# All weight remainders in one GpSimd loop, and the 31-tap convolution with 13 taps on TensorE and its diagonals made on ScalarE

## The reference, cut to what matters

```python
def conformer_conv(x, pw1_w, pw1_b, dw_w, dw_b, ln_g, ln_b, pw2_w, pw2_b):
    h = x @ pw1_w + pw1_b
    a, g = jnp.split(h, 2, axis=-1)
    h = a * jax.nn.sigmoid(g)
    h = causal_dwconv(h, dw_w, dw_b)      # depthwise, 31 taps
    h = layer_norm(h, ln_g, ln_b)
    h = jax.nn.silu(h)
    return h @ pw2_w + pw2_b

def conv_gated_ffn(x, w_up, w_gate, conv_w, conv_b, w_down):
    u = x @ w_up
    g = causal_dwconv(x @ w_gate, conv_w, conv_b)   # depthwise, 3 taps
    return (jax.nn.silu(g) * u) @ w_down
```

## Time and profile before

| what | value |
| --- | --- |
| median of 3 executions | 2216.51 us (2215.62 to 2216.83) |
| the profiled execution | 2214.47 us |
| its span, first to last instruction | 2212.7 us |
| TensorE matmul busy | 2047.4 us, 93% |
| VectorE busy | 1145.1 us, 52% |
| ScalarE busy | 716.4 us, 32% |
| GpSimd busy | 146.0 us, 7% |
| mean granted TensorE clock | 0.964 |

### The profile page before, as it was taken

One profiled execution on the slowest core, in us unless ns is written; L12 is line 12 of the kernel. 1 busy time (PEld: TensorE's weight loads), 2 busy tenths in 40 slices (PEclk: granted clock), 3 DMA queues, 4 the chain that ended last, 5 costly groups with the idle time before them and its releaser, 6 DMA issues.

```text
span 2212.7 us, 22972 instructions
## 1 busy us (share of the span) xinstructions
PE 2047.4 (93%) x8878; PEld 1604.9 (73%) x8878; DVE 1145.1 (52%) x1315; ACT 716.4 (32%) x793; POOL 146.0 (7%) x200
## 2 busy tenths in 40 slices
PE   2998999999999699679999999989999999999996
PEld 0874678877788477456888888758777778888884
DVE  6674333225533799765455553354366545555433
ACT  2423233235422311145222231154365342222222
POOL 0000000000000388500000000000000000000000
PEclk8898999999999899889999999989999999999998
DMA  7211122221122011111222223212200222222221
GB/s 312 77 58 38 56 77 96 95 95 39 41 100 107 19 57 57 48 57 56 77 96 96 103 104 108 101 51 102 76 1 18 88 76 85 103 97 95 102 107 38
DMA packets 24831, 177.55 MB, mean 80 GB/s; under 512 B 2752, under 2 KB 2880, under 8 KB 4288
## 3 DMA queue, kind: packets, MB, share of 16 engines
q1 hardware_dynamic: 23040, 160.95, 20.4%
q10 hardware_dynamic: 1728, 15.73, 1.7%
HBM read 174.57 MB, written 2.10 MB: 80 GB/s over the span
## 4 chain that ended last, share of the span: by engine, by line
PE 81%; DVE 8%; issue 4%; ACT 4%; POOL 2%; DMA 1%; DVEq 0%; ACTq 0%; SPq 0%; POOLq 0%
PE PS L423 22%; PE PS L424 21%; PE PS L425 21%; PE PS L498 3%; PE PS L778 2%; POOL DG L390 2%; PE PS L788 2%; PE PS L489 1%; PE PS L488 1%; PE PS L487 1%; DVE WL L1157 1%; PE PS L606 1%; DVE ADAS L1225 1%; DVE TT L1180 1%; DMA SWR<-w_small 1%
## 5 line engine op out<-in xcount | busy, mean ns | idle before, releaser
L423 PE MATMUL PS<-H,WH 128*128 128x512 f32 x1552 | 614.2, 396 | 24.8 <-DVE L L1185 14.0
L424 PE MATMUL PS<-L,WH 128*128 128x512 f32 x1552 | 608.4, 392 | 0.0
L425 PE MATMUL PS<-H,WL 128*128 128x512 f32 x1552 | 608.0, 392 | 0.0
L1157 DVE TENSOR_TENSOR WL<-RAW,WH 128x2048 fp32r<-128x2048 f32 x149 | 341.3, 2290 | 325.7 <-ACT WH L817 325.2
L817 ACT ACTIVATE WH<-RAW 128x2048 fp32r<-128x2048 f32 x149 | 284.5, 1909 | 282.6 <-PE PS L425 238.0
L423 PEld LDWEIGHTS PS<-H,WH 128*128 128x128 f32 x1552 | 294.2, 190 | 94.0 <-issue 25.3
L425 PEld LDWEIGHTS PS<-H,WL 128*128 128x128 f32 x1552 | 293.9, 189 | 62.4
L424 PEld LDWEIGHTS PS<-L,WH 128*128 128x128 f32 x1552 | 294.1, 190 | 60.0 <-issue 0.2
L390 POOL TENSOR_SCALAR DG<-IDENT,DWC 128x128 fp32r<-128x128 f32 x176 | 142.6, 829 | 773.2 <-DVE DWC L1517 773.2
L423 PE MATMUL PS<-FH,WH 128*128 128x512 f32 x352 | 136.9, 389 | 0.0
L424 PE MATMUL PS<-FL,WH 128*128 128x512 f32 x352 | 136.9, 389 | 0.0
(11 more groups left out here) (284 smaller groups left out, 2622.6 us busy)
## 6 DMA issues: line engine op xcount, KB each, us to landing
RAW<-w SPq DMA_DIRECT2D x149, 1024.0 KB, 4.8
ADA<-w_ada ACTq DMA_DIRECT2D x8, 1536.0 KB, 23.8
X<-x_t SPq DMA_DIRECT2D x1, 2048.0 KB, 15.1
PWR<-w_ple ACTq DMA_DIRECT2D x2, 1024.0 KB, 4.8
out<-X SPq DMA_DIRECT2D x8, 256.0 KB, 2.2
PR<-p_t ACTq DMA_DIRECT2D x2, 512.0 KB, 5.9
PAR<-par SPq DMA_DIRECT2D x1, 334.0 KB, 7.0
SWR<-w_small SPq DMA_DIRECT2D x1, 160.0 KB, 18.8
```

Source lines behind the costliest of these rows:

```text
L423: nc.tensor.matmul(ps, wh, xh, start=start, stop=False)
L424: nc.tensor.matmul(ps, wh, xl, start=False, stop=False)
L425: return nc.tensor.matmul(ps, wl, xh, start=False, stop=stop)
L1157: v.tensor_tensor(WL[:, p], RAW[:, p], WH[:, p].bitcast(F32), ALU.subtract).then_inc(w_lo, 1)
```

## The change

The remainders of all 149 slots move from VectorE to GpSimd, in one loop that waits for the high part and subtracts. Nothing else runs on GpSimd behind its constants. The diagonals move from GpSimd to ScalarE, as activations with the weight column as scale, ahead of the slot's sigmoid; they are 26 a group now, as TensorE takes 13 taps and VectorE 18. The copy `DWC` is gone, and `CVB` and `DW` lie elsewhere.

```diff
-PE_TAPS = 11
+PE_TAPS = 13
...
-            def diagonals(s):
-                p = s.odd()
-
-                pool.wait_ge(dwc_ready, s.val(1, 1))
-                for part in range(2):
-                    for k in range(PE_TAPS):
-                        ins = nc.gpsimd.tensor_scalar(DG[:, p, part, k, :], IDENT[:], DWC[:, p, part, k:k + 1], None,
-                                                      ALU.mult)
-                ins.then_inc(dg_ready, 1)
-            for m in range(KC):
-                diagonals(Step(m))
+            def split_lo(g, p):
+                pool.wait_ge(w_hi, g + 1)
+                nc.gpsimd.tensor_tensor(WL[:, p], RAW[:, p], WH[:, p].bitcast(F32), ALU.subtract).then_inc(w_lo, 1)
+
+            with pool.Fori(0, NSLOTS // 2) as t:
+                for i in range(2):
+                    split_lo(2 * t + i, i)
+            for g in range(NSLOTS // 2 * 2, NSLOTS):
+                split_lo(g, g % 2)
...
+            def diagonals(s):
+                p = s.odd()
+                if not (isinstance(s.val(), int) and s.val() < 2):
+                    act.wait_ge(cp_ps, s.val(1, -1))
+                for part in range(2):
+                    for k in range(PE_TAPS):
+                        m = s.val(1, k * KC)
+                        w_ = DW[:, part, m:m + 1] if isinstance(m, int) else DW[:, part, bass.ds(m, 1)]
+                        ins = a(DG[:, p, part, k, :], IDENT[:], ACT.Identity, scale=w_.bitcast(F32))
+                ins.then_inc(dg_ready, 1)
+
             def pw1(s, p):
+                if isinstance(s.val(), int) and s.val() == 0:
+                    act.wait_ge(dw_lo, 1)
+                diagonals(s)
                 gates("pw1", KC, "pw1_b")(s, p)
...
-            slots("pw1", pw1)
+            slots("pw1", pw1, head=2)
...
             def slots(stage, body, per=0, tail=0, head=0):
-                g0 = SLOT0[stage]
-
-                def one(s):
-                    split_lo(s, 1, g0 + 1)
-                    body(s, s.odd(1, GROUP0[stage]))
-                steps(dve, own, COUNT[stage], per, one, tail=tail, head=head)
+                steps(dve, own, COUNT[stage], per, lambda s: body(s, s.odd(1, GROUP0[stage])), tail=tail, head=head)
...
-                v.tensor_copy(DWC[:, q].unsqueeze(3), dw[:, :, :, m:m + 1] if isinstance(m, int) else
-                              dw[:, :, :, bass.ds(m, 1)]).then_inc(dwc_ready, 1)
```

More of the change, by code:

```diff
@@ L218, in build @@
         DG = at("DG", A + 36, [P, 2, 2, PE_TAPS, P], F32R)
-        CVB = at("CVB", A + 60, [P, 1, T])
-        DW = at("DW", A + 62, [P, 2, PE_TAPS * KC], F32R)
-        DWC = at("DWC", A + 66, [P, 2, 2, PE_TAPS])
+        CVB = at("CVB", A + 62, [P, 1, T])
+        DW = at("DW", A + 64, [P, 2, PE_TAPS * KC], F32R)
         HCH = at("HCH", A + 68, [P, 2, PAD + T], F32R)
@@ L314, in build @@
         mg_ready, mg_hi, mg_lo = sem("mg_ready"), sem("mg_hi"), sem("mg_lo")
-        hc_hi, hc_lo, dw_hi, dwc_ready, dg_ready, cp_ps = (sem(s) for s in (
-            "hc_hi", "hc_lo", "dw_hi", "dwc_ready", "dg_ready", "cp_ps"))
+        hc_hi, hc_lo, dw_hi, dw_lo, dg_ready, cp_ps = (sem(s) for s in (
+            "hc_hi", "hc_lo", "dw_hi", "dw_lo", "dg_ready", "cp_ps"))
         sele_ready = sem("sele_ready")
@@ L1150, in _ @@
             acc, tmp = TT[:, 2, :], TT[:, 3, :]
[L1152 to L1157, removed]
-            def slots(stage, body, per=0, tail=0, head=0):
-                g0 = SLOT0[stage]
-                def one(s):
-                    split_lo(s, 1, g0 + 1)
-                    body(s, s.odd(1, GROUP0[stage]))
-                steps(dve, own, COUNT[stage], per, one, tail=tail, head=head)
+            def slots(stage, body, per=0, tail=0, head=0):
+                steps(dve, own, COUNT[stage], per, lambda s: body(s, s.odd(1, GROUP0[stage])), tail=tail, head=head)
             def evacuated(s, stage, mul=1, more=0):
@@ L1230, in _ @@
                         own.did(ins)
-            split_lo(Step(0), 1, 0)
             def modulation(part):
@@ L1287, in _ @@
             v.scalar_tensor_tensor(E, U, -1.0, U, ALU.mult, ALU.min).then_inc(dt_u, 1)
-            split_lo(Step(0), 1, SLOT0["q"] + 1)
             dve.wait_ge(dt_e, 1)
@@ L1373, in _ @@
             dve.wait_ge(cb_ready, 2)
-            split_lo(Step(1), 1, SLOT0["q"] + 1)
             seg(0)
             for h in range(SSM_HEADS):
-                if h % KC == 1:
-                    split_lo(Step(2 + h // KC), 1, SLOT0["q"] + 1)
                 if h + 1 < SSM_HEADS:
@@ L1392, in _ @@
             dve.wait_ge(y_used, KC)
-            slots("z", lambda s, p: None)
             for j in range(COUNT["k"]):
-                split_lo(Step(j), 1, SLOT0["k"] + 1)
                 if j == 0:
@@ L1409, in _ @@
             slots("ssm_out", ssm_out)
-            slots("v", lambda s, p: None)
             n = NT * FOX_HEADS
@@ L1428, in _ @@
             for i in range(n + 1):
-                if i % KC == 2:
-                    split_lo(Step(i // KC), 1, SLOT0["za"] + 1)
                 if i < n:
@@ L1491, in _ @@
             dve.wait_ge(dw_hi, 1)
-            own.did(v.tensor_tensor(DW[:, 1, :], col("dw_w", 0, PE_TAPS * KC), DW[:, 0, :].bitcast(F32), ALU.subtract))
-            own.settle()
+            v.tensor_tensor(DW[:, 1, :], col("dw_w", 0, PE_TAPS * KC), DW[:, 0, :].bitcast(F32),
+                            ALU.subtract).then_inc(dw_lo, 1)
             own.did(v.memset(acc, 0.0))
@@ L1513, in pw1 @@
                 cv, hc = rows(CV, s.val(), 1), rows(HC, s.val(), 1)
-                q, m = s.odd(), s.val()
-                dw = DW[:].bitcast(F32).rearrange("p a (k m) -> p a k m", m=KC)
-                v.tensor_copy(DWC[:, q].unsqueeze(3), dw[:, :, :, m:m + 1] if isinstance(m, int) else
-                              dw[:, :, :, bass.ds(m, 1)]).then_inc(dwc_ready, 1)
+                q = s.odd()
                 dsts = (cv, CVB[:])
@@ L1639, in down_one @@
                 def down_one(s):
-                    for part in range(DOWN_S):
-                        split_lo(s, DOWN_S, SLOT0[down] + part + 1)
                     added(down, DOWN_S, DOWN_S - 1)(s, s.odd(1, GROUP0[down]))
@@ L1672, in _ @@
             slots("k1", k1_lo, head=COUNT["k1"])
-            slots("v1", lambda s, p: None)
             for i in range(SB_HEADS + 2):
```

## The result

The changed kernel takes 2245.68 us (median of 4 runs, 2241.38 to 2246.04), the kernel before 2216.07 (4 runs on the same chip, 2215.51 to 2216.83). The ratio is 1.0129, 95% interval 1.0111 to 1.0146: slower, by 29.6 us where 11.8 were forecast. The profiled execution has a span of 2244.3 us against 2212.7, at a granted clock of 0.959 of full speed against 0.964.

A forecast was written before the change was run, and what follows sets the result against it. TensorE, with a matmul in flight for 93% of the span, was taken as the bound, `pw1` as paced by VectorE. Terms of 15.4 + 3.8 + 4.4 + 4.6 + 2.3 - 18.7 = +11.8 us gave 2228 us, range 2204 to 2256.

The forecast's parts named there:

- Step 6: All other stages, including attention and state-space heads: no change; if the cover fails, 1 to 3 us at some five places.
- Term 1: `up0` and `up1`: remainder ready 0.7 us after the need, once in two slots, over 44 slots: +15.4 us.
- Terms 2 and 4: Later remainders delay TensorE: `xbc` +3.8 us; second slots of `gate0` and `gate1` +4.6 together, of `q1` +2.3.
- Term 3: The start: GpSimd's subtraction takes its turn amid VectorE's modulation sums, which wait: +4.4 us.
- Term 5: `pw1`: VectorE's group falls from 21.1 to 19.8 us and the wait for GpSimd's diagonals goes: -18.7 us.
- -32: `pw1`: the change in us at which TensorE bounds the stage, if GpSimd's turn is shorter or does not hold VectorE.
- Rival 1: GpSimd's subtraction takes under 4.1 us, so the `up` stages cost nothing at 3.8: 2203 us, chance 0.2.
- Rival 2: The subtraction takes 4.5 us but does not hold VectorE throughout; TensorE bounds `pw1`: 2214 us, chance 0.13.
- Rival 3: GpSimd needs 5.3 us or more, or ScalarE's diagonals over 0.6 us each: 2256 us and up, chance 0.14.
- the forecast's 2217 to 2246: Whole kernel, for a GpSimd subtraction of 4.2 to 5 us: 2217 to 2246 us, chance 0.5.
- 35 us for each us: Whole kernel: each us of GpSimd's subtraction time moves the sum by 35 us, as long as it is above 3.8.

The follow-up runs named there:

- e3: e1 with only the remainders of two slots in the state-space heads (q3 and z0) moved to GpSimd: 2198.03 us, ratio 0.9922.
- e10: e3 with GpSimd subtracting only 8 of 16 tiles in those two slots, the other halves keeping old values: 2190.8 us, ratio 0.9885.
- e2: e1 with the remainders of the 44 slots made in `up0` and `up1` moved to GpSimd: 2214.78 us, ratio 0.9995.
- e7: e2 with GpSimd subtracting only 8 of a slot's 16 tiles, the others keeping old values: 2192.48 us, ratio 0.989.
- e11: e1 with 11 taps on TensorE instead of 13, all remainders on VectorE: 2193.62 us, ratio 0.9895.
- e5: The changed kernel with GpSimd's loop begun only after VectorE's modulation sums: 2239.31 us, ratio 1.0095.
- e1: The changed kernel's convolution half alone: 13 taps on TensorE, diagonals on ScalarE, all 149 remainders on VectorE: 2189.94 us, ratio 0.9881.
- e4: e1 with only the eight remainders made in `pw1` moved to GpSimd: 2200.64 us, ratio 0.9931.
- e6: e1 with only the remainders made in `gate0` and `gate1` moved to GpSimd: 2196.9 us, ratio 0.9907.

## Why the prediction was wrong

The direction, the hold and the place of most of the loss were right; the size was not. By its own steps:

- **Step 6, "All else at nothing", failed.** It let the state-space part's held operations "stand in front of a TensorE that has queued matmuls". The queue is shorter than the hold: in the changed kernel and in e3 TensorE waits 2.8 us for the held product and then loses 2.9 at the low clock, so that one hold costs 5.7 us (the changed kernel's stretch is 6.6 longer). The bound was named, 1 to 3 us at each of some five places, and taken as zero. e10 shows that it is the length of the turn: at 2.39 us all but 0.6 is gone.
- **Term 1, `up0` and `up1`, was mis-sized**: +15.4 forecast, +22.7 measured; e2 alone has +22.5. The mechanism stood: a delay per pair of slots, and only above the room (e7). But it is 1.07 us instead of 0.7. The subtraction is 4.60 us and not 4.5, and the two hand-overs take 0.08 and 0.13 instead of 0.1 together, so the product comes 0.9 after the need; and after a wait the second matmul comes 0.33 after the first instead of 0.23, in both slots. A few tenths of a microsecond, 22 times.
- **Terms 2 and 4 had the wait and not what follows it.** `xbc` +5.6 instead of +3.8, of which the low clock gives 1.7; the gates +6.2 instead of +4.6. Both waits grew by 2.3, as forecast; behind them the low clock took 2.8 more than before in `gate0` and 1.1 less in `gate1`. As e10 and e11 have the same 2.8 in `gate0` without the longer wait, this part can't be put down to the change. `q1` came out at +2.3 exactly. `xbc` was not tried alone, so its part rests on the trace.
- **Term 3, the start**: +4.7 against +4.4, and e5 takes it away, 4.7 us by the stage.
- **Term 5, `pw1`**: -20.0 against -18.7. The pace of 19.7 against 19.8 and the diagonals' 0.297 against 0.30 hold. The pace is in part luck: the parts that the text takes off 21.1 us sum to 5.5 and leave 15.6, not 15.3. The runs have 15.3 (17.5 in e1 less the 2.2 of the remainder), since without GpSimd's diagonals the taps come every 0.66 us instead of 0.78, more than the 0.09 a tap that was taken off. The two halves of the term are now separate: -26.2 for the convolution (e1), +6.2 for the turn of 4.6 us (e4). With no turn, e1 is at TensorE's 20.0 a group in its second half, so the "-32" of the text looks too much; its own case, with VectorE free of the remainders too, was not run.
- **Rival 1, a GpSimd under 4.1 us**, falls by every row of the subtraction. **Rival 2, no hold**, falls by the start, by `pw1` and by e3. **Rival 3** asked for 5.3 us or more: beside VectorE's taps it is 5.0 to 5.1 in the changed kernel (up to 5.5 in the gates, 7.0 once in `pw2`), 4.71 in the mean, and no stage was bound by ScalarE.
- **That 2245.7 lies inside the forecast's 2217 to 2246 is luck.** The upper end stood for a subtraction of 5 us. By the prediction's own rule, 35 us for each us, the measured 4.60 to 4.71 would give 2232 to 2235.

Between the profiled executions the sum was short by 19.8 us (31.6 less 11.8): 7.3 are term 1, 6.6 the heads of step 6, 3.4 terms 2 and 4, and 2.5 what is left of all other stretches. By the medians it was short by 17.8. The -3.0 of the attention and the +3.1 from `q1` to `wo` were not explained; they nearly cancel. Of the second, 1.3 lie in the third and fourth slots of `q1`, in `k1` and in the first slots of `v1`, and come back in e5 alone, the other kernel with all remainders on GpSimd. The rest lies in the attention behind them, which takes 129.0 to 133.1 us from kernel to kernel without such remainders.

## What to carry to other kernels

To move work to a slower idle engine is decided by the room between input and need, at each site: 4.6 us where there are 3.9 costs about 1 us 22 times, 2.4 us costs nothing. Count in that room the semaphore hops and the first matmul after a wait. Then list every two-operand SBUF instruction of VectorE that can meet the long one and has TensorE behind it: "TensorE has work queued" is to be counted in microseconds against the hold. Look at what the same slots do in kernels that leave them alone before a difference is called an effect. A change of two halves is to be tried as two: one gained 26 us here and hid behind a loss of 56.

## What the runs showed of the hardware

- A GpSimd subtraction of 128 x 2048 takes 4.60 us alone, 5.0 to 5.1 beside VectorE's taps (mean of `pw1`'s eight 4.95), and 2.39 for 1024 columns. A two-operand VectorE instruction that meets it is held to its end (0.74 to 5.12, 0.68 to 3.43, 3.41 to 7.65 us), and so is GpSimd by VectorE: at the start it waited 3.4 us and let two operations pass. An operation with one operand in PSUM was not held (0.69 us). The Trainium skill (SBUF — State Buffer, section Who interferes with whom) has this as an exclusive lock; the trace agrees.
- ScalarE makes a 128 x 128 diagonal from a column of scales every 0.297 us (26 in 7.71).
- A wait of TensorE can cost more than its length, and how much can't be told from the length: 1.7 us more at 1.2 GHz behind 3.24 us in `xbc` and nothing behind 3.4 two slots earlier; 2.9 behind 2.8 in the heads; in `gate0` nothing behind 3.04 before, 2.8 behind 3.1 in e11, 2.8 behind 5.3 in the changed kernel and 1.3 behind 5.3 in e6.
